# A chunked RWKV-7 recurrence: the 128x128 block inverse rebuilt from 32x32 TensorE tiles

## What is computed

```python
def step(S, inp):
    r_t, w_t, k_t, v_t, kk_t, a_t = inp
    sa = jnp.einsum('bhvk,bhk->bhv', S, -kk_t)
    S = (S * w_t[:, :, None, :]
         + sa[..., None] * (kk_t * a_t)[:, :, None, :]
         + v_t[..., None] * k_t[:, :, None, :])
    return S, jnp.einsum('bhvk,bhk->bhv', S, r_t)
```

## Time and profile before

| | us |
|---|---|
| median of 3 runs | 1325.6 (1325.56 to 1328.6) |
| the profiled execution | 1324.9 |
| its span, first to last instruction | 1323.0 |
| PE busy in it | 1275.8 |
| DVE busy in it | 853.1 |
| ACT busy in it | 479.3 |
| POOL busy in it | 254.3 |

### The profile page before, as it was taken

How to read it: one execution, slowest core, us unless ns; L and a number is a source line. 1 busy time by engine, 2 the same in 40 slices (tenths; PEclk the granted TensorE clock), 3 DMA queues, 4 the chain that set the end, 5 groups by cost and what they waited for, 6 DMA issues and landing times.

```text
span 1323.0 us, 18110 instructions
## 1 busy us (share of the span) xinstructions
PE 1275.8 (96%) x6973; PEld 1057.7 (80%) x6973; DVE 853.1 (64%) x1308; ACT 479.3 (36%) x847; POOL 254.3 (19%) x196
## 2 busy tenths in 40 slices
PE   7999999989899999999999999999999999999996
PEld 6888888655698888888878888888888888888885
DVE  6865623399778787744476656566777676546765
ACT  6100032488422232234363333333333334333334
POOL 0476600034300000000003331332233200000001
PEclk9999999999999999989999999999999999999998
DMA  5576532200322333333214123214544567766643
GB/s 222 173 246 232 207 121 92 104 2 17 80 71 71 75 103 94 115 123 127 80 48 127 52 93 96 83 62 159 175 141 162 191 222 293 250 210 209 210 140 135
DMA packets 117232, 179.05 MB, mean 135 GB/s; under 512 B 30368, under 2 KB 59040, under 8 KB 116896
## 3 DMA queue, kind: packets, MB, share of 16 engines
q1 hardware_dynamic: 117152, 177.96, 41.0%
HBM read 123.90 MB, written 53.49 MB: 134 GB/s over the span
## 4 chain that ended last, share of the span: by engine, by line
PE 88%; DVE 7%; issue 2%; DMA 2%; ACT 2%; POOL 0%; DVEq 0%; SPq 0%; ACTq 0%; POOLq 0%
PE bank L2317 28%; PE bank L369 21%; PE bank L2417 15%; PE bank L1400 4%; PE bank L474 2%; PE bank L383 2%; PE bank L1271 1%; PE bank L1527 1%; PE bank L1485 1%; PE bank L1479 1%; DVE scores L1178 1%; PE bank L992 1%; PE bank L1497 1%; PE bank L1514 1%; PE bank L1501 1%
## 5 line engine op out<-in xcount | busy, mean ns | idle before, releaser
L2317 PE MATMUL bank<-thi,ahi 128*128 128x512 f32 x320 | 124.5, 389 | 0.0
L2317 PE MATMUL bank<-tlo,ahi 128*128 128x512 f32 x320 | 124.5, 389 | 0.0
L2317 PE MATMUL bank<-thi,alo 128*128 128x512 f32 x320 | 124.5, 389 | 0.0
L2417 PE MATMUL bank<-ch,dwh 128*128 128x512 f32 x308 | 120.3, 391 | 0.6 <-DVE dwl L1995 0.6
L2417 PE MATMUL bank<-ch,dwl 128*128 128x512 f32 x308 | 119.9, 389 | 0.0
L2417 PE MATMUL bank<-cl,dwh 128*128 128x512 f32 x308 | 119.8, 389 | 0.0
L348 DVE TENSOR_TENSOR ring_wlo<-ring_raw,ring_whi 128x1024 fp32r<-128x1024 f32 x30 | 40.6, 1352 | 121.9 <-ACT ring_whi L342 121.9
L369 PE MATMUL bank<-hhi,ring_whi 128*128 128x512 f32 x288 | 114.4, 397 | 0.0
L369 PE MATMUL bank<-hhi,ring_wlo 128*128 128x512 f32 x288 | 112.2, 390 | 0.0
L369 PE MATMUL bank<-hlo,ring_whi 128*128 128x512 f32 x288 | 112.1, 389 | 0.0
L2317 PE MATMUL bank<-x1hi,ahi 128*128 128x512 f32 x240 | 93.4, 389 | 0.0
(11 more groups left out here) (336 smaller groups left out, 2862.2 us busy)
## 6 DMA issues: line engine op xcount, KB each, us to landing
hraw<-hid_scratch SPq DMA_DIRECT2D x12, 1024.0 KB, 5.7
hid_scratch<-hid SPq DMA_DIRECT2D x22, 512.0 KB, 6.1
hid_scratch<-rt SPq DMA_DIRECT2D x11, 1024.0 KB, 4.7
dwr<-down_sums SPq DMA_DIRECT2D x16, 704.0 KB, 4.2
ring_raw<-in_w_in SPq DMA_DIRECT2D x20, 512.0 KB, 4.3
raw_a<-in_w_gate_up SPq DMA_DIRECT2D x20, 512.0 KB, 4.4
raw_b<-in_w_gate_up SPq DMA_DIRECT2D x20, 512.0 KB, 5.2
dwr<-in_w_down SPq DMA_DIRECT2D x12, 704.0 KB, 4.1
```

Source lines behind the costliest of these rows:

```text
L2317: mm = pe.matmul(b[:, :], w[:, k, :], m[:, k, :], start=opens and k == 0 and i == 0, stop=not (j, n) in parts and k == 3 and i == 2, skip_ ...
L2417: mm = pe.matmul(b[:, :], w[m % 2][:, k, :], a[:, k, :], start=opens and k == 0 and i == 0, stop=name not in PART2 and k == KF - 1 and i = ...
```

## The change

Level 1 and level 2 no longer multiply 128x128 matrices. A helper, `blocks_of`, issues one product for each head and each 32-row group: a 32x32 piece of the matrix is the stationary operand, 16 or 32 columns are streamed, and the result goes to 32 partitions of one PSUM bank. `X` and `XT` shrink to 64 columns for each head (the 64-block on whose rows a partition lies) and are read from DRAM by two transfers each, one for each half of the partitions. The products of a tile become: t1 (8 heads x 4 groups, 16 columns), y1 (8 x 4, 32 columns), x1 (8 x 2, 16 columns, which brings `X` up to date and replaces transposes and ACT's copy), t2 (8 x 2, 32 columns) and y2 (8 x 2, 32 columns). DVE masks t1 with one column of constants (`C_PAIR + 2`) in one instruction, adds x1 and y1 in one each, and copies y2 in two of 32 partitions. ACT copies t2.

PE's order: in tiles 1 to 6 corners(1), R, updates(1), the first half of O, corners(2), the second half of O, `outputs(t - 1)`, updates(2), `cumulative(t + 2)`, U and the rest as before; in tiles 0 and 7 R and the first half of O stand ahead of corners(1). ACT copies R low and t2 ahead of `exponentials`. DVE's masked copy of b(t + 1) moves from the end of tile t - 1 to behind the first instruction of tile t. The values of a tile are read into one of two buffers (`vtk_`), ahead of gather and scatter. Bank numbers change to suit (kt goes to bank 2, where U is too; b2 to bank 3). No products are added to keep PE busy.

In stage 8 three quarters of the last block of results are transposed ahead of the seventh k step of the last product, instead of ahead of the next to last, and ACT squares these while PE goes on (`square_three`), so that one quarter (128 columns) is left at the end (`square_last`).

```diff
-        Ts1, Ts2 = at("Ts1", 104, [P, H, P]), at("Ts2", 108, [P, H, P])
-        X, XT = at("X", 112, [P, H, P]), at("XT", 116, [P, H, P])
+        Ts1, Ts2 = at("Ts1", 104, [P, H, 32]), at("Ts2", 108, [P, H, 32])
+        X, XT = at("X", 112, [P, H, HD]), at("XT", 116, [P, H, HD])
...
-        sgt, vtk = at("sgt", 188, [P, W]), at("vtk", 190, [P, W])
+        sgt, vtk_ = at("sgt", 188, [P, W]), [at("vtk0", 190, [P, W]), at("vtk1", 105, [P, W])]
...
-            order5 += [("t10", t, 0), ("t11", t, 6), ("y10", t, 4), ("y11", t, 5)]
+            order5 += [("t1", t, 1), ("R", t, 0), ("O", t, 5), ("y1", t, 4), ("x1", t, 6), ("t2", t, 2)]
             order5 += [("ot", t - 1, 7)] if t else []
-            order5 += [("x10", t, 2), ("x11", t, 3)] + plan_cum(t + 2)
-            order5 += [("t20", t, 0), ("t21", t, 6), ("y20", t, 4), ("y21", t, 5)]
-            order5 += [("R", t, 0), ("O", t, 5), ("U", t, 2)]
+            order5 += [("y2", t, 4)] + plan_cum(t + 2) + [("U", t, 2)]
...
-                sp.dma_start(X[:, :, :], bass.AP(d_i.tensor, P, [[2 * P, P], [8 * IMG2, H], [1, P]])).then_inc(s_xl, 16)
-                if t:
-                    C.result(sp, "U", t - 1)
-                sp.dma_start(XT[:, :, :], bass.AP(d_i.tensor, 0, [[2 * P, P], [8 * IMG2, H], [1, P]])).then_inc(s_xt, 16)
+                for m, o, done in ((X, P, s_xl), (XT, 0, s_xt)):
+                    if t and m is XT:
+                        C.result(sp, "U", t - 1)
+                    for q in range(2):
+                        sp.dma_start(m[q * HD:(q + 1) * HD, :, :],
+                                     bass.AP(d_i.tensor, o + q * (2 * P + 1) * HD, [[2 * P, HD], [8 * IMG2, H], [1, HD]])
+                                     ).then_inc(done, 16)
...
+                    sp.wait_ge(s_vtk, 16 * t + 16)
+                    if t:
+                        C.result(sp, "S", t - 1)
+                    sp.dma_start(vtk_[(t + 1) % 2][:, :], v_dram[tok(t + 1), :]).then_inc(s_vtk, 16)
                     gather(t + 1)
                     scatter(t + 1)
-                    C.result(sp, "S", t)
-                    sp.dma_start(vtk[:, :], v_dram[tok(t + 1), :]).then_inc(s_vtk, 16)
...
-            def transposed(job, g, t):
-                b = C.claim(pe, f"{job}{g}", t)
-                for j in range(4):
-                    mm = pe.transpose(b[:, j * P:(j + 1) * P], XT[:, 4 * g + j, :], ident)
-                C.done(mm, f"{job}{g}", t)
+            def blocks_of(b, count, lhs, rhs, groups):
+                n = len(groups) * H
+                for h in range(H):
+                    for g in groups:
+                        lo, ro = lhs(g, h), rhs(g, h)
+                        to = g[2]
+                        mm = pe.matmul(b[32 * to:32 * to + 32, h * count:(h + 1) * count] if len(ro.shape) == 2 else
+                                       b[32 * to:32 * to + 32, h * count:(h + 1) * count].rearrange("p (a w) -> p a w", a=2),
+                                       lo, ro, start=h == 0, stop=h == H - 1, skip_group_check=True)
+                return mm
+            def rows(g):
+                return slice(32 * g, 32 * g + 32)
+            FOUR = [(g, g % 2, g) for g in range(4)]
             def corners(n, t):
-                for g in range(2):
-                    b = C.claim(pe, f"t{n}{g}", t)
-                    if n == 1:
-                        pe.wait_ge(s_xl, 16 * t + 16)
-                    else:
-                        C.emptied(pe, f"x1{g}", t)
-                    C.done(four(b, g, lambda h: NB[t % 2][:, h, 1, :], lambda h: X[:, h, :]), f"t{n}{g}", t)
+                if n == 1:
+                    b = C.claim(pe, "t1", t)
+                    pe.wait_ge(s_xl, 32 * t + 32)
+                    C.done(blocks_of(b, 16, lambda g, h: NB[t % 2][rows(g[0]), h, 1, rows(g[0])],
+                                     lambda g, h: X[rows(g[0]), h, 32 * g[1]:32 * g[1] + 16], FOUR), "t1", t)
+                else:
+                    b = C.claim(pe, "t2", t)
+                    C.emptied(pe, "x1", t)
+                    C.done(blocks_of(b, 32, lambda g, h: NB[t % 2][rows(g[0]), h, 1, rows(g[2])],
+                                     lambda g, h: X[rows(g[0]), h, 0:32], [(0, 0, 1), (2, 0, 3)]), "t2", t)
             def updates(n, t):
-                m = Ts1 if n == 1 else Ts2
-                for g in range(2):
-                    C.emptied(pe, f"t{n}{g}", t)
-                    b = C.claim(pe, f"y{n}{g}", t)
-                    C.done(four(b, g, lambda h: m[:, h, :], lambda h: XT[:, h, :]), f"y{n}{g}", t)
+                C.emptied(pe, f"t{n}", t)
+                if n == 1:
+                    b = C.claim(pe, "y1", t)
+                    C.done(blocks_of(b, 32, lambda g, h: Ts1[rows(g[0]), h, :],
+                                     lambda g, h: XT[rows(g[0]), h, :].rearrange("p (a w) -> p a w", a=2)[:, :, 16:32], FOUR),
+                           "y1", t)
+                    b = C.claim(pe, "x1", t)
+                    C.done(blocks_of(b, 16, lambda g, h: XT[rows(g[0]), h, 0:32],
+                                     lambda g, h: Ts1[rows(g[0]), h, 0:16], [(0, 0, 0), (2, 0, 2)]), "x1", t)
+                else:
+                    C.emptied(pe, "y1", t)
+                    b = C.claim(pe, "y2", t)
+                    C.done(blocks_of(b, 32, lambda g, h: Ts2[rows(g[0]), h, :],
+                                     lambda g, h: XT[rows(g[0]), h, 32:64], [(1, 0, 0), (3, 0, 2)]), "y2", t)
...
-                corners(1, t)
-                pe.wait_ge(s_xt, 16 * t + 16)
-                updates(1, t)
-                if t:
-                    outputs(t - 1)
-                for g in range(2):
-                    C.emptied(pe, f"y1{g}", t)
-                    transposed("x1", g, t)
-                if t + 2 < NT:
-                    cumulative(pe, t + 2)
-                corners(2, t)
-                updates(2, t)
+                vtk, ends = vtk_[t % 2], t in (0, NT - 1)
+                def products_of(b, part, *hs):
+                    for h in hs:
+                        mm = pe.matmul(b[:, h * HD:(h + 1) * HD], KB[:, h, part, :], vtk[:, h * HD:(h + 1) * HD],
+                                       start=part == 0 and h == 0, stop=False, skip_group_check=True)
+                    return mm
+                if not ends:
+                    corners(1, t)
+                br = C.claim(pe, "R", t)
                 if t:
                     pe.wait_ge(s_S, t)
                 pe.wait_ge(s_vtk, 16 * t + 16)
                 for g in range(4):
                     C.emptied(pe, f"k{g}", t)
-                br = C.claim(pe, "R", t)
                 for p in range(NP):
                     pe.matmul(br[:, p * P:(p + 1) * P], alpha(t, p), S[:, p, :], start=p == 0, stop=False,
                               skip_group_check=True)
-                for h in range(H):
-                    mm = pe.matmul(br[:, h * HD:(h + 1) * HD], KB[:, h, 1, :], vtk[:, h * HD:(h + 1) * HD],
-                                   start=False, stop=False, skip_group_check=True)
...
+                products_of(br, 1, *range(H)).then_inc(s_r, 1)
+                if ends:
+                    bo = C.claim(pe, "O", t)
+                    products_of(bo, 0, *range(4))
+                    corners(1, t)
+                pe.wait_ge(s_xt, 32 * t + 32)
+                updates(1, t)
+                if not ends:
+                    bo = C.claim(pe, "O", t)
+                    products_of(bo, 0, *range(4))
+                corners(2, t)
+                products_of(bo, 0, *range(4, H))
+                if t:
+                    outputs(t - 1)
+                updates(2, t)
+                if t + 2 < NT:
+                    cumulative(pe, t + 2)
...
                 b = C.result(act, job, t)
-                C.read(act.activation(dst, b[rows, :], ACT.Copy), job, t)
-            def keep_x(job, t):
-                for g in range(2):
-                    keep(f"{job}{g}", t, row(X[:, 4 * g:4 * g + 4, :]))
+                C.read(act.activation(dst, b[rows, 0:cols], ACT.Copy), job, t)
...
-                keep_x("x1", t)
-                if last:
+                    C.result(act, "x1", t)
                     mix_high(act, 1)
-                if t + 2 < NT:
-                    exponentials(act, t + 2, 0, 1)
-                if last:
                     mix_high(act, 2)
                 act.wait_ge(s_r, t + 1)
                 act.activation(rs_[low, :], bank[0][low, :], ACT.Copy).then_inc(s_rlow, 1)
+                keep("t2", t, row(Ts2[:, :, :]), cols=32 * H)
+                if t + 2 < NT:
+                    exponentials(act, t + 2, 0, 1)
...
+            def first_corners(t):
+                b = C.result(dve, "t1", t)[:, 0:16 * H].rearrange("p (h n) -> p h n", h=H)
+                C.read(dve.tensor_scalar(Ts1[:, :, 0:16], b, cst[:, C_PAIR + 2:C_PAIR + 3], None, ALU.mult), "t1", t)
+            def first_updates(t):
```

(42 more changed lines are left out.)

57 lines of the change are left out of this document (18 added, 39 removed).

## The result

The changed kernel takes 1360.5 us (median of 4 runs, 1358.4 to 1362.2), the kernel before beside it 1326.2. The ratio is 1.0254, its interval 1.0234 to 1.0275: slower by 34 us, where I had forecast 1317.5 and a gain of 8. The profiled execution spans 1357.8 us.

What follows compares the result with a forecast made beforehand. PE's work and a loop through all engines were taken as equally long bounds, 28.5 us a tile. Terms -2.5 + 0 - 0.7 - 3.9 - 1.0 = -8.1 took 1324.9 to 1316.8, median 1317.5; own range 1312 to 1321, 8-in-10 range 1309 to 1340.

Steps and rivals of the forecast that it cites:

- What PE saves: Block inverse: 224 small records replace 72, costing 3.2 us instead of 9.3; PE's need per tile falls from 27.5 to about 22.
- The rule cited there: Inverse's products: different row tiles cannot access the same PSUM bank at once, so the four row groups' overlap would be lost.
- second rival: Inverse: one bank, no overlap, 0.035 us per record throughout, inverse 7.8 us; +26 us, 1351; chance 0.12.
- the low end of the price: Inverse's small records at best overlap, 0.009 and 0.0175 us each: 2.5 us for the inverse.
- The loop at full clock: Middle tile: 11.1 us to `prepare`, 9.7 for `prepare` and `lanes`, 7.1 transfers: 27.9 against 28.4, -0.5 five times, -2.5.
- The third rival: PE's clock falls once in each middle tile, stretching dense products by up to 3 us a tile: 1335; chance 0.14.
- Against: the small products are followed by 2.7 us of dense R: Middle tiles: sign against the clock falling, as 2.7 us of dense R follow the small products.
- Tile 7, -3.9: End of `lanes` to U in tile 7 shrinks from 22.9 us to 18.2 to 19, X's landing off the path: -3.9.
- Stage 8, -1.0: Stage 8: squares of 512 columns at 0.6 us become 128 columns at about 0.3 on the last chain: -1.0.

Runs made afterwards that it cites:

- The runs of 32 rows, products and fillers: Kernel before, corners and updates contracted over 32 rows instead of 128: 1423.5 us. Changed kernel, fillers (overwritten products) of 32 rows in PE's longer idle stretches: 1380.6 us.
- fillers over all rows: Changed kernel with dense products of 256 to 512 columns, results overwritten, in every longer idle stretch of PE: 1338.6 us.
- run with most fillers: Changed kernel, DVE's next-NB masks ahead of first corners, next tile's `lanes` ahead of `prepare`, dense overwritten products, including 512 columns ahead of t2, 384 ahead of y1: 1321.3 us.
- with the conversions behind the copies: As the run with most fillers, but in tile 7 DVE's `mlo` conversions behind the inverse's last update and two fillers ahead of U instead of seven: 1320.3 us.
- run with lanes early: Changed kernel with DVE's masks of the next NB ahead of its first corners and next tile's `lanes` ahead of `prepare`, no fillers: 1343.3 us.
- runs with dense fillers: Changed kernel with overwritten products over all rows where PE idles: 1338.6 us; with `lanes` ahead of `prepare` too, 1324.2 with some, 1321.3 with more.
- The same program: Changed kernel with `lanes` ahead of `prepare` and some dense overwritten products, 384 columns ahead of t2 in most tiles, none ahead of X: 1324.2 us.

## Why the prediction failed, point by point

**What PE saves: right.** Four row groups of 32x32 overlap, also into one bank: t1 0.73 us (0.7 forecast), y1 and x1 1.2 together (1.3), t2 and y2 0.69 each (0.6). The rule cited there, of the Trainium skill, TensorEngine Tiling (Array Packing), Gotcha 1, speaks of one bank; at the second rival's price t1 would have been 2.2 us. No such loss is in this trace, and that rival falls with it. Two slips in the working don't touch the forecast: the low end of the price, 0.009 and 0.0175, gives 2.8 us for the inverse and not 2.5, and the row of 16 products with 256 columns gives 0.101 per start, (1.89 - 0.38) / 15, and not 0.108.

**The loop at full clock: right.** From tile 1: `prepare` starts at 397.62, 10.9 us into the tile (11.1 forecast), held by the exponentials as said; `lanes` ends 9.7 later; X releases PE 7.3 behind that (7.1). The tile is 27.9 (27.9).

**The third rival: the failed step.** It was there with chance 0.14 and said that the clock falls once in each middle tile; the forecast itself put the clock at nothing. The rival priced it at up to 3 us a tile. The one fall in the trace of before lasted 6.9 us and ended in dense work:

```profile
569.90:576.80 6.90, 6.34 (x23) 5.77 (x24) 4.17 (x6) 4.08 (x5) 0.00 (x0) 0.51 0.27 76
```

"Against: the small products are followed by 2.7 us of dense R" took it that dense work beside them keeps the clock. Measured: tiles 2 and 4 +8.2 and +8.4 against 27.9, tile 5 +0.3; tile 0 32.0 instead of 27.2, +4.8; tile 6 34.2 instead of 25.1, +9.1; tile 7 30.8 instead of 20.7, +10.1. That is 40.9 of the 43 us by which the time missed (in tile 7 part of it is no matter of the clock, below). The term was short by the length of the stretch, 20 to 34 us instead of 6.9; and in counting PE's idle time as cover I did not ask what PE's 23 us of work become when slowed: 36, past the loop of 28. The rival had tiles 0, 6 and 7 at nothing, and more than half of the loss is there.

**Why it stays down** I had no view for. PE's busy share says nothing here. The runs of 32 rows, products and fillers, show that products over few rows are part of the cause, and fillers over all rows win most of it back. R and O put back gave 23 us, with falls of 6.8 to 10.2 us in tiles 0 to 5, but 27 and 31 us in tiles 6 and 7 with the same block of R and O: what ends a stretch stays open.

**Tile 7, -3.9: 2.4 seen with another order, nothing in the change.** PE waits 3.59 us ahead of U at 595.53, behind the last of these on DVE:

```profile
592.31 2.35 DVE L1304 TENSOR_TENSOR mlo<-mix,mhi 128x1024 fp32r<-128x1024 f32 x2
594.58 0.41 DVE L1626 COPY XT<-bank 32x256 f32<-32x256 f32 x1
595.00 0.42 DVE L1627 COPY XT<-bank 32x256 f32<-32x256 f32 x1
```

I had counted them, and hoped for 19 us from the end of `lanes` to U. With the clock mostly up (run with most fillers) it is 22.5 (538.65 to 561.17, seven fillers in it), as long as before; with the conversions behind the copies 20.5 (536.42 to 556.95). So, by these two runs, nearly nothing of the 3.9 was to be had in the change's own order of these, and 2.4 in the other; how much the fillers ahead of U hide stays open.

**Stage 8, -1.0: as forecast in the trace, not to be seen in time.** The squares take 0.28 us for 0.60, and from the end of DVE's last addition of `c` to the end of the span it is 9.6 us, before 10.6. In the profile of the run with stage 8 alone it is 10.2.

```profile
1347.54 0.69 DVE L2545 TENSOR_TENSOR c<-c,q 128x512 f32<-128x512 f32 x1
1348.65 0.28 ACT L2460 ACTIVATE fin<-bank 128x128 f32<-128x128 f32 x1 [3.67 <-PE bank L2372]
```

## What to carry to other kernels

Cutting products to small tiles saves PE's time and uses less of the array; where PE still has to work on through the stretch, ask what clock it will have, and look at how many rows the products use, not only at PE's busy share. In this kernel it was better by 23 us to put R and O in one block behind the small ones than between them, though the same block did not help in its last two tiles. Before relying on idle time as slack, multiply PE's busy time by two. A gain at full clock that leaves PE idle (27.9 us, 4 idle) is worth less than one that lets the next loop go faster (24.9 us, 2 idle), and overwritten dense products can be a cheap way to keep it.

## What the runs showed of the hardware

- PE busy without a pause can have half a clock for 41 us (kernel before, 32 rows), and a wait of 4.1 to 5.1 us cost 6.8 us of it when 128x128 products follow.
- 64 float32 records of 32x32 with 16 columns, four row groups in turn into one bank, take 0.73 us at full clock, 0.011 each, and 1.05 at half.
- Within stretches of small products PE sometimes stops for nothing that the profile shows. In tile 0 of the changed kernel, in the middle of x1, and the clock fell inside this stop, at 360.3:

```profile
361.19 0.51 PE L1408 MATMUL bank<-Ts,XT 32*32 32x16 f32 x13 [1.61 <-issue]
```

  In the run with lanes early it was 1.19 us within O, just ahead of a fall at 456.2. In the runs with dense fillers most of the falls that are left follow such stops, of 0.5 to 2.3 us. What causes them was not tried.
- The same program differed by 20 us between executions on one chip (1315.1 to 1334.8), in step with its mean clock (0.991 to 0.974).
